# Decode attention over paged rows: one lookup and two transfers per cached page, issued by pairs, with the rope keys gathered from the rows and turned on chip

## The reference

```python
ckv = jnp.concatenate([cache_ckv_l[pages].reshape(past, KV_LORA), ckv_new], axis=0)   # 2048 + 8 rows of 256
kpe = jnp.concatenate([cache_kpe_l[pages].reshape(past, QK_ROPE), kpe_new], axis=0)   # 2048 + 8 rows of 32
k_nope = jnp.einsum('...lc,chd->...lhd', c_kv, w_uk)                                  # 8 heads of 64
k = rmsnorm(jnp.concatenate([k_nope, k_rope], axis=-1), k_head_norm)                  # k_rope: kpe, the same for all heads
s = jnp.einsum('qhd,khd->hqk', q, k) * SCALE                                          # then causal mask, softmax p
o_lat = jnp.einsum('hqk,kc->qhc', p, c_kv)
```

## Time and profile before

| | |
|---|---|
| median of 3 runs | 1536.07 us (1535.14 to 1537.04) |
| the profiled execution, its own time | 1533.52 us |
| span of that execution, first to last instruction | 1531.5 us |
| mean granted TensorE clock | 0.994 of 2.4 GHz |
| decode loop, first page product to last key scores | 706.8 to 1017.5 us |
| products of TensorE, instructions | 10771 |
| transfers on SP's queue | 139.97 MB in 244498 packets |

### The profile page before, as it was taken

The page is one execution under the profiler, slowest core; times in us unless marked ns, Lnnn a source line. Parts: engine busy times, 40 slices in busy tenths (PEclk is TensorE's granted clock), DMA queues, the critical chain, the costliest instruction groups (busy, mean ns, idle before and its releaser), DMA issues.

```text
span 1531.5 us, 31143 instructions
## 1 busy us (share of the span) xinstructions
PE 1491.3 (97%) x10771; PEld 1434.9 (94%) x10771; DVE 1067.9 (70%) x1738; ACT 655.5 (43%) x1215; POOL 454.3 (30%) x463
## 2 busy tenths in 40 slices
PE   8999999999999999999999888999999999999999
PEld 8999999999999999588888888888999999999999
DVE  7999898421269975865888788854759998985000
ACT  6444445322221242464666666642434444445111
POOL 4000002454465744320344333223551000005432
PEclk9999999999999999999999999999999999999999
DMA  6233234222333651003444443432222332332322
GB/s 176 70 103 103 82 97 116 78 83 75 82 83 100 83 116 47 13 4 99 129 127 129 124 125 111 128 106 72 83 83 56 109 97 85 106 92 81 91 77 82
DMA packets 245460, 141.69 MB, mean 93 GB/s; under 512 B 22705, under 2 KB 242290, under 8 KB 245362
## 3 DMA queue, kind: packets, MB, share of 16 engines
q1 hardware_dynamic: 244498, 139.97, 33.1%
q10 hardware_dynamic: 864, 0.48, 0.1%
HBM read 136.82 MB, written 3.58 MB: 92 GB/s over the span
## 4 chain that ended last, share of the span: by engine, by line
PE 52%; issue 24%; SPq 11%; POOL 7%; DVE 3%; ACT 1%; DMA 1%; POOLq 0%; DVEq 0%; ACTq 0%
PE ps L493 28%; PE ps L1522 14%; POOL w_lobuf L468 7%; SPq L726 3%; SPq L731 3%; SPq L742 3%; SPq L737 2%; PE ps L1861 2%; PE ps L1647 1%; PE ps L1701 1%; PE ps L1676 1%; PE ps L479 1%; PE ps L1691 1%; DMA w_rawbuf<-in_ffn_w_gu 1%; DVE cT_lo L2466 1%
## 5 line engine op out<-in xcount | busy, mean ns | idle before, releaser
L468 POOL TENSOR_TENSOR w_lobuf<-w_rawbuf,w_hibuf 128x256 fp32r<-128x256 f32 (+1 forms) x328 | 316.4, 996 | 801.4 <-ACT w_hibuf L461 801.3
L1522 PE MATMUL ps<-xs,w 128*128 128x288 f32 x3192 | 427.7, 296 | 0.8 <-DVE w L1984 0.8
L1522 PEld LDWEIGHTS ps<-xs,w 128*128 128x128 f32 x3192 | 426.8, 188 | 1.5 <-issue 1.5
L461 ACT ACTIVATE w_hibuf<-w_rawbuf 128x1024 fp32r<-128x1024 f32 (+1 forms) x89 | 104.4, 1173 | 353.3 <-PE ps L493 332.9
L2192 DVE SCALAR_TENSOR_TENSOR xT<-ps,xT 128x576 f32<-128x576 f32 x23 | 17.4, 756 | 202.4 <-PE ps L493 202.4
L1984 DVE TENSOR_TENSOR w<-w_raw,w 128x512 fp32r<-128x512 f32 x228 | 154.0, 690 | 0.3 <-ACT w L1029 0.2
L493 PE MATMUL ps<-a_hi,w_lobuf 128*128 128x288 f32 x682 | 147.5, 297 | 0.0
L493 PE MATMUL ps<-a_hi,w_hibuf 128*128 128x288 f32 x682 | 147.2, 296 | 0.0
L493 PE MATMUL ps<-x_hi,w_hibuf 128*128 128x288 f32 x656 | 142.2, 298 | 4.1 <-POOL w_lobuf L468 2.9
L493 PE MATMUL ps<-a_lo,w_hibuf 128*128 128x288 f32 x682 | 145.5, 294 | 0.0
L493 PE MATMUL ps<-x_lo,w_hibuf 128*128 128x288 f32 x656 | 140.8, 296 | 0.0
(11 more groups left out here) (335 smaller groups left out, 2602.6 us busy)
## 6 DMA issues: line engine op xcount, KB each, us to landing
w_raw<-in_ffn_w_gu SPq DMA_DIRECT2D x76, 256.0 KB, 2.9
up_rows<-in_ffn_w_gu SPq DMA_DIRECT2D x72, 256.0 KB, 3.2
c_nat<-in_pages_in SPq DMA_DIRECT2D x128, 144.0 KB, 2.2
c_ring<-in_pages_t SPq DMA_DIRECT2D x128, 128.0 KB, 2.1
w_rawbuf<-in_w_in SPq DMA_DIRECT2D x58, 256.0 KB, 3.2
w_rawbuf<-in_ffn_w_down SPq DMA_DIRECT2D x32, 384.0 KB, 4.0
w_rawbuf<-in_ffn_w_down SPq DMA_DIRECT2D x32, 320.0 KB, 3.4
w_rawbuf<-in_ffn_w_gu SPq DMA_DIRECT2D x24, 256.0 KB, 3.4
```

The lines of the kernel that those rows point to most:

```text
L461: act.activation(w_hibuf[:, r % HIS, 0:size], w_rawbuf[:, r, 0:size], ACT.Copy).then_inc(w_hi_done, 1)
L468: ins = pool.tensor_tensor(w_lobuf[:, r, part], w_rawbuf[:, r, part], w_hibuf[:, r % HIS, part].bitcast(F32), ALU.subtract)
L1522: mm = pe.matmul(ps[:, seven_bank(f, slot), 0:HALF], m, xs[:, slot, n, k, :], start=k == 0 and j == 0, stop=k == KH - 1 and j == 2)
```

## The change

SP's `load_pages` by groups becomes `load_pair` by pairs: two lookups, two ring issues, two row issues. The ring issue of pair pp waits for the low part of pair pp-2, the row issue for the pair's own use count. The transposed rope keys are no longer an input, and their 128 transfers go. Sequence 0 keeps the page numbers that it has looked up: 16 lookups for 16 pages.

Instead, VectorE copies the rope values of a group's four pages out of `c_nat` into `kpe_rows` (128 x 128), behind the two sums of iteration 2g; TensorE transposes them behind page 4g+2 (behind page 3 in the first group of sequence 0) into bank `PEB`; ScalarE copies them into `kpeT` behind the squares of that page; the key scores wait for that copy. GpSimd's squaring of a sequence waits for the last of its four gathers. The counts of the semaphores follow.

```diff
-        def kpe_page(s, g):
-            return 3 if at(s, g) == (0, 0) else 4 * g + 1
+        def kpe_page(s, g):
+            return 3 if at(s, g) == (0, 0) else 4 * g + 2
...
-            def load_pages(s, b, used=None):
-                for g in range(NP // 4):
-                    found = [page_of(s, 4 * g + u) for u in range(4)]
-                    sp.wait_ge(ct_lo, s * PAIRS + (2 * g - 2))
-                    load_ring(g, found)
-                    sp.wait_ge(pe_scored, s * (NP // 4) + (g - 1))
-                    load_kpe(g, found)
-                    if used is not None:
-                        sp.wait_ge(pages_used, used + 2 * (g + 1))
-                    load_rows(b, g, found)
...
+            def load_ring(pp, two):
+                for u, page in enumerate(two):
+                    sp.dma_start(c_ring[:, (2 * pp + u + RING // 2) % RING, :], pages_t[ds(page, 1), :, :].rearrange("a p c -> (a p) c")).then_inc(ring_in[pp % 2], 16)
+            def load_rows(b, pp, two):
+                for u, page in enumerate(two):
+                    sp.dma_start(c_nat[:, b, 2 * pp + u, :], pages_in[ds(page, 1), :, :].rearrange("a p c -> (a p) c")).then_inc(nat_in[b][pp // 2], 16)
+            def load_pair(s, b, pp, used=None):
+                two = [page_of(s, 2 * pp + u) for u in range(2)]
+                sp.wait_ge(ct_lo, s * PAIRS + (pp - 1))
+                load_ring(pp, two)
+                if used is not None:
+                    sp.wait_ge(pages_used, used + (pp + 1))
+                load_rows(b, pp, two)
...
             sp.wait_ge(rows_done, 2 * NT + PT_TILES)
+            early = [[page_of(0, 2 * pp + u) for u in range(2)] for pp in range(2)]
+            for pp in range(2):
+                load_ring(pp, early[pp])
             sp.wait_ge(prep_q, 1)
+            for pp in range(2):
+                load_rows(0, pp, early[pp])
+            later = [[page_of(0, 2 * pp + u) for u in range(2)] for pp in range(2, 4)]
+            for pp in range(2, 4):
+                load_rows(0, pp, later[pp - 2])
             sp.wait_ge(prep_tr, 2)
             sp.wait_ge(uk_split, 1)
+            for pp in range(2, 4):
+                sp.wait_ge(ct_lo, pp - 1)
+                load_ring(pp, later[pp - 2])
+            for pp in range(4, PAIRS):
+                load_pair(0, 0, pp)
             sp.wait_ge(prep_mm, 2)
+            for pp in range(PAIRS):
+                load_pair(1, 1, pp)
             with sp.Fori(1, NS // 2) as i:
                 for b in range(2):
+                    for pp in range(PAIRS):
+                        load_pair(i * 2 + b, b, pp, i * (2 * PAIRS) + (EARLY_PAIRS + PAIRS * (b - 2)))
...
                 for g in range(NP // 4):
                     pool.wait_ge(nat_in[b][g], uses * 64)
+                pool.wait_ge(kpe_row, s * 4 + 4)
                 k = c_nat[:, b, :, KL:KL + DR]
...
+            def kpe_copy(s, g):
+                act.wait_ge(pe_tr, s * 4 + (g + 1))
+                if not (isinstance(s, int) and s == 0 and g < 2):
+                    act.wait_ge(pe_scored, s * 4 + (g - 1))
+                act.activation(kpeT[:, g % 2, :], ps[:, PEB, 4 * HQ:4 * HQ + P], ACT.Copy).then_inc(pe_copied, 1)
...
                         act.activation(sq[:, u, 0:H * DN].rearrange("p (g c) -> p g c", g=2), ps[:, n:n + 2, k_cols(b)], ACT.Square).then_inc(page_sq, 1)
+                        if t == kpe_page(s, t // 4):
+                            kpe_copy(s, t // 4)
...
+            def kpe_transpose(s, b, g, uses):
+                pe.wait_ge(kpe_row, s * 4 + (g + 1))
...
+                    pe.wait_ge(scores_read, s * 4 + g)
+                pe.transpose(ps[:, PEB, 4 * HQ:4 * HQ + P], kpe_rows[:, :, :].rearrange("p t d -> p (t d)"), ident[:, :]).then_inc(pe_tr, 1)
             def kpe_scores(s, g):
-                pe.wait_ge(kpe_in[g % 2], (s * 2 + (g // 2 + 1)) * 64)
...
+                pe.wait_ge(pe_copied, s * 4 + (g + 1))
...
                         mm.then_inc(page_mm, 1)
                         if prev and stacked(s) and t == NP - 1:
                             next(soft)
+                        if t == kpe_page(s, g):
+                            kpe_transpose(s, b, g, uses)
...
+                    if pp % 2 == 0:
+                        g = pp // 2
+                        dve.wait_ge(nat_in[b][g], uses * 64)
+                        if not (isinstance(s, int) and s == 0 and g == 0):
+                            dve.wait_ge(pe_tr, s * 4 + g)
+                        dve.tensor_copy(kpe_rows[:, :, :], c_nat[:, b, 4 * g:4 * g + 4, KL:KL + DR]).then_inc(kpe_row, 1)
                     if pp % 2:
                         g = pp // 2
                         dve.wait_ge(pe_scored, s * 4 + (g + 1))
```

More of the change, by code:

```diff
@@ L91, in constants, with layer @@
     return {"ident": ident, "causal": causal, "rope": rope, "new_mask": new}
-def layer(nc, x_t, cols_in, pages_t, pages_in, pages_k, state_conv, page_table, w, const, out):
+def layer(nc, x_t, cols_in, pages_t, pages_in, state_conv, page_table, w, const, out):
     ctx = ExitStack()
@@ L223, in layer @@
         c_ring = place("c_ring", [P, RING, KL], F32, S3)
+        kpe_rows = place("kpe_rows", [P, 4, DR], F32, ring_at + 8 * DK * P + 8192 + 8 * (SQ + KN + SQ))
         kpeT = place("kpeT", [P, 2, P], F32, rstd_at)
@@ L726, in page_of @@
                 return sp.value_load(pages[0:1, ds(s * NP + t, 1)], min_val=0, max_val=pages_t.shape[0] - 1)
[L728 to L737, removed]
@@ L739, in load_kpe @@
[L739 to L754 removed]
+            def load_ring(pp, two):
+                for u, page in enumerate(two):
+                    sp.dma_start(c_ring[:, (2 * pp + u + RING // 2) % RING, :], pages_t[ds(page, 1), :, :].rearrange("a p c -> (a p) c"))\
+                        .then_inc(ring_in[pp % 2], 16)
@@ L756, in _ @@
             sp.wait_ge(rows_done, 2 * NT + PT_TILES)
-            found = [page_of(0, u) for u in range(4)]
-            load_ring(0, found)
-            load_kpe(0, found)
+            early = [[page_of(0, 2 * pp + u) for u in range(2)] for pp in range(2)]
+            for pp in range(2):
+                load_ring(pp, early[pp])
             sp.wait_ge(prep_q, 1)
-            load_rows(0, 0, found)
-            for g in (1, 2):
-                load_rows(0, g, [page_of(0, 4 * g + u) for u in range(4)])
+            for pp in range(2):
+                load_rows(0, pp, early[pp])
@@ L764, in _ @@
+            later = [[page_of(0, 2 * pp + u) for u in range(2)] for pp in range(2, 4)]
+            for pp in range(2, 4):
+                load_rows(0, pp, later[pp - 2])
             sp.wait_ge(prep_tr, 2)
             sp.wait_ge(uk_split, 1)
-            found = [page_of(0, 4 + u) for u in range(4)]
-            load_ring(1, found)
-            load_kpe(1, found)
-            load_rows(0, 3, [page_of(0, 12 + u) for u in range(4)])
-            for g in (2, 3):
-                found = [page_of(0, 4 * g + u) for u in range(4)]
-                sp.wait_ge(ct_lo, 2 * g - 2)
-                load_ring(g, found)
-                sp.wait_ge(pe_scored, g - 1)
-                load_kpe(g, found)
+            for pp in range(2, 4):
+                sp.wait_ge(ct_lo, pp - 1)
+                load_ring(pp, later[pp - 2])
@@ L2750, in laid_out @@
     return {"x_t": rows.T, "cols_in": np.concatenate([*gains, taps], axis=1), "pages_t": pages_t,
-            "pages_in": np.concatenate([ckv, kpe], axis=2), "pages_k": kpe.transpose(0, 2, 1)}
+            "pages_in": np.concatenate([ckv, kpe], axis=2)}
 def state_first(state):
```

16 lines of the change are left out of this document (7 added, 9 removed).

## The result

| | before | after |
|---|---|---|
| median, runs of one chip | 1535.61 us (1533.72 to 1537.04) | 1558.83 us (1557.57 to 1562.40) |
| ratio to before | | 1.0156, 95% interval 1.0134 to 1.0177 |
| span of the profiled execution | 1531.5 us | 1558.1 us |
| mean granted TensorE clock | 0.994 | 0.990 |

The account below looks back on a forecast made before the run. SP's always-busy queue was not taken as the bound: most TensorE waits came from other engines. Costs of 19.3 us less gains of 10.2 gave +9.1 on the median 1536.07, so 1545.2 us; range 1528 to 1556.

Parts of the forecast that it names:

- SP really was the bound: Rival: SP's queue bounds the decode loop; decides if VectorE gathers before page 4g+2 ends on TensorE; 1529 us, chance 0.2.
- SP's relief: Decode loop: SP, with fewer issues, stops being late, and TensorE waits led back to it go; gain 10.2 us.
- fold waits: TensorE's two long waits for the fold, 2.08 and 1.80 us, shrink to 0.6 each; gain 2.7 us.
- half clock: Slow TensorE products at 1.2 GHz behind the first long fold wait (833 to 870 us) go; gain 1.2 us.
- small waits: Small TensorE waits behind late ring pages elsewhere in the loop go; gain estimated at 1.0 us.
- Its wait shrinks by 3 us ... 5.3 us: Sequence 7: ScalarE's merge-weight wait shrinks 3 us; TensorE's 3.1 us den_sum wait and 2.2 us of half clock go.
- my 994.4: Sequence 7: forecast time, in us, when SP issues the first merge weights, instead of 995.91.
- The stalls in sequences 1 to 6: TensorE waits before transposes for VectorE's gather, behind the sums: 2.7 us a sequence, 16.2 in all.
- For sequences 1 to 6 I take the same: Extends the 2.7 us of stalls to all six sequences; layer-norm in 5 and 6 delays VectorE but TensorE's present waits are larger.
- third rival: Slower by more: two stalls a sequence bring TensorE's 1.2 GHz level, 8.4 us more, 1554 us, chance 0.12.
- Sequence 7: only g=1, 1.5: In the last sequence only group 1's transpose stalls TensorE, waiting for its gather; cost 1.5 us.
- the rule: VectorE copies share ports with GpSimd: a gather could wait over 1 us, only g=3 near; some 3 us, outside the sum.

Follow-up runs that it names:

- experiment 3: Changed kernel without gather, transposes and copy-out, keys zero, SP still issuing by pairs: 1529.11 us, ratio 0.9956 to the kernel before.
- experiment 6: Kernel before, SP by groups, without its rope-key transfers and TensorE's wait for them, keys zero: 1527.61 us, ratio 0.9943.
- experiment 5: Kernel before, with ScalarE's split of the first merge weight one iteration later in the last sequence: 1530.28 us, ratio 0.9972.
- experiment 1: Changed kernel with VectorE's gather moved to the head of its iteration, right behind the low part: 1544.71 us, ratio 1.0057.
- Experiment 2: Changed kernel with ScalarE's split of the first merge weight one iteration later in sequence 7, gather unmoved: 1552.08 us, ratio 1.0104.
- 8: Changed kernel, early gather, transposes and copies-out one page earlier, split unmoved, SP issuing first merge weights behind pair 4 of sequence 7: 1538.46 us.
- 4: Changed kernel with both the gather at the head of its iteration and the merge-weight split one iteration later: 1536.20 us, ratio 1.0002.
- 7: Changed kernel with early gather, later merge-weight split, and all transposes and copies-out one page earlier: 1537.93 us, ratio 1.0012.
- 9: Changed kernel, early gather, later merge-weight split, transposes and copies-out one page earlier except group 1's: 1537.22 us, ratio 1.0003.
- experiment 11: Changed kernel, early gather, later merge-weight split, but gathers alone: no transposes or copies-out, keys zero: 1535.00 us, ratio 0.9991.
- 12: Changed kernel, later split, transposes and copies-out one page earlier except group 1's, no gathers, rows to be turned zero: 1530.66 us, ratio 0.9972.
- 10: Changed kernel without gather, transposes and copy-out, keys zero, and the merge-weight split one iteration later: 1527.64 us, ratio 0.9944.

## Why the prediction was right in sign and wrong in size

**What bounds the kernel: right, and shown.** SP's queue held 70% of the chain, yet emptying it gained 6.6 us (experiment 3) or 8.7 (experiment 6), not a tenth of the loop. The rival "SP really was the bound" (1529 us) fails on its own condition: VectorE had not gathered in time.

**SP's relief: 6.6 us instead of 10.2.** The parts outside sequence 7 (fold waits 2.7, half clock 1.2, small waits 1.0: 4.9) measured 4.1 us: sequences 1 to 6 take 232.0 us before and 227.9 in experiment 3. In sum they were nearly right, but not one by one. The fold wait of 2.08 us in sequence 3 fell to 0.54, and its half clock went; that of 1.80 in sequence 5, which I had called the same, stayed at 1.65 without any key issue, so its 1.2 us were no gain: sequence 5 took 41.3 us before and 41.1 in experiment 3.

The step that failed is "Its wait shrinks by 3 us ... 5.3 us". I let SP issue the weight right behind low part 5. In experiment 3 low part 5 is done at 989.53 and the weight leaves at 994.35, because pair 6 and the lookups of pair 7 hold SP. That this is 0.05 us from my 994.4 is luck: mine was in the time of the kernel before (and its own terms, 991.3 + 2.1 + 1.5, give 994.9), and against the end of sequence 6 the weight left no earlier than before (24.9 us, 24.7). I also let ScalarE arrive later by delays that were themselves costs. The wait went from 6.06 only to 5.13, and sequence 7 gained 1.9 us. In the changed kernel, with those delays, it was 3.90, near my 3, and den_sum's wait did go; the copy-out's, 6.29, came in its place. The size of the prize was right (experiment 5), its cause was not in the change.

**The hop on TensorE, VectorE and ScalarE as work: right.** In the changed kernel the gather took 0.22 us (forecast 0.25), the transpose 0.27 to 0.33, the copy-out 0.27 (0.31).

**The stalls in sequences 1 to 6.** The mechanism is shown by experiment 1: move the gather, and they go. The places and sizes:

| group | forecast | sequence 3 |
|---|---|---|
| 0 | about 0, absorbed | 0.57 |
| 1 | 1.5 | 1.47 |
| 2 | about 0, absorbed | 1.52 |
| 3 | 1.1 | 1.27 |

Against the kernel without keys, sequences 1 to 4 cost 2.5 us each, where 2.7 were forecast. The stalls sum to 4.8; about half took the place of waits that were there before. So the total was right though two of four terms were set to zero: their waits are real, and the waits they displaced paid for them; that this came out at the forecast is luck in part. That they cost nothing by themselves can't be read from this; the sum of 2.5 is what is shown.

**Sequences 5 and 6: 3.5 and 4.4 us instead of 2.7 each.** "For sequences 1 to 6 I take the same" failed. I had named the layer-norm work on VectorE and offset it against "TensorE's present waits". In sequence 5 it stands straight ahead of the gather:

```profile
917.33 0.85 DVE L2571 TENSOR_TENSOR ln_acc<-ln_acc,y 128x576 f32<-128x576 f32 x1
918.10 1.27 DVE L2655 TENSOR_REDUCE page_ss<-sq 128x8 f32<-128x512 f32 x2
919.29 0.21 DVE L2663 COPY kpe_rows<-c_nat 128x128 f32<-128x128 f32 x1
```
```profile
919.56 0.33 PE L1826 MATMUL ps<-ident,kpe_rows 128*128 128x128 f32 x1 [2.29 <-DVE kpe_rows L2663]
```

2.29 is the 1.47 of the other sequences plus these 0.85, and behind it the granted clock is 0.63 from 920 to 923 us. That is the third rival (1554, chance 0.12), in two sequences of seven: the windows of 0.86 over 12 us in 5 and 0.88 over 14 us in 6 are 3.4 us each at 1.2 GHz.

**Sequence 7 is the failure: +7.1 where -3.8 was forecast, 10.9 of the 13.1 us that the loop was off.** 3.4 is the merge weight's gain that did not come; 7.4 is the key path, which cost 8.9 us against experiment 3 where "Sequence 7: only g=1, 1.5" was written. Three of its four groups stalled, 1.57, 1.83 and 1.01 us before the transposes at 998.06, 1007.04 and 1015.86. Softmax steps or not, the sums of the iteration alone keep the gather late. And I put the merge split and the copy-out in separate paragraphs and never in one list. The copy-out belongs to page 10, the split stands behind page 9, on the same engine; the rows that show its 6.06 us wait were on my table, and I asked only which wait the change would shorten, not which instruction it would now put behind it. Experiment 2 gives 6.7 us for that alone. It is also an interaction: the same late weight costs 5.6 us in the trace where the next pair's high part is what matters behind it (experiment 5), and nothing where SP issues it early (8).

**Smaller terms.** Sequence 0: 1.2 us against 1.6. "GpSimd's squaring now waits ...: nothing" holds, though GpSimd waited 27.7 us in all: no engine is shown waiting for these squares.

**Gather and GpSimd.** The sum left out that a gather could wait for a GpSimd instruction. In the changed kernel it happened to one of 32. VectorE's timeline and GpSimd's in sequence 5:

```profile
941.03 0.74 DVE L2663 COPY kpe_rows<-c_nat 128x128 f32<-128x128 f32 x1
941.69 0.68 DVE L2475 TENSOR_TENSOR cT_lo<-c_ring,cT_hi 128x512 fp32r<-128x512 f32 x1
```
```profile
939.35 2.34 POOL L928 TENSOR_TENSOR c_lo<-c_nat,c_hi 128x512 fp32r<-128x512 f32 x2 [1.23 <-ACT c_hi L1324]
941.94 1.33 POOL L956 TENSOR_TENSOR c_nat<-c_nat 128x512 f32<-128x512 f32 x1 [0.25 <-DVE kpe_rows L2663]
```

The gather that began beside the subtraction took 0.74 us instead of 0.22, and ended 0.08 us after it; one at 858.28, begun 0.08 after such a pair's end, took 0.21. This agrees with the Trainium skill ("SBUF — State Buffer", "Who interferes with whom"), by which a VectorE copy can contend with GpSimd for the ports that they share. In the changed kernel it cost 0.5 us once, where I had priced the rule at some 3. With the gather moved (experiments 1, 4, 7 to 9 and 11) six or seven of the 32 took 1.2 us, some 6 to 7 us more on VectorE: twice the price that I had put on the rule, and nearly all in group 1, not in group 3, where I had placed it.

**What stays open.** The early gather costs 7.4 us by the medians. The collision with GpSimd and the wait for the maximum behind it are read from the traces, but no run takes them away: a gather placed early and clear of the subtraction was not tried. The wide spread of experiment 11 (8 us between its runs) goes with the granted clock of the whole run: 0.998 in the run of 1530.65 us, 0.992 in that of 1538.58. The difference is 2 x 0.006 x 1536 = 18 us more at 1.2 GHz, which can cost up to 9 us, an estimate. Why one execution gets more of it than another stays open.

## What to carry to other kernels

When work moves onto an engine's hand-written list, write out for each moved instruction all that stands ahead of it in every peeled or special iteration, and ask of each wait in the list what new instruction comes to stand behind it: here 0.27 us of copying behind a 3.9 us wait cost 6.7 us. A queue that is always busy and fills the chain of waits may still be worth only half a per cent; leave the suspected work out and time it before replacing it. And judge a fix by the time, not by the wait it removes: waits on the key path fell from 14.8 to 4.2 us between two kernels of equal time. Then look again at how long the moved instruction itself takes in its new place: here 1.2 us instead of 0.22, once in each of six sequences.

## What the runs showed of the hardware that was not expected

- The length of a wait did not decide by itself whether TensorE's clock fell. Four waits of 0.57 to 1.52 us in 40 us left the granted clock at 1.00 (823 to 863 us after, 35.1 us busy of 40); one of 2.29 was followed by 0.63 for the next 3 us, and one of 6.29 by 0.74 over 20 us. But before the fold of sequence 5, waits of 1.54 to 1.71 us were followed by 3.4 us at 1.2 GHz in experiments 1, 4, 7, 8, 9, 11 and 12 (0.79 over 8 us in each), and waits of 1.65 (3), 1.66 (10) and 1.80 us (before) were not. The 2.08 us before the fold of sequence 3 brought it in the kernel before, and 2.31 us at the same place in experiment 5 did not (1.00 from 850 to 870 us):

```profile
854.18 0.38 PE L1790 MATMUL ps<-o_lat,fold 128*128 128x1 f32 x2 [2.31 <-DVE o_lat L2532]
```

- A VectorE copy of 128x128 values, rows of 32 strided out of four pages, takes 0.22 us, as long as the copy of 64 columns did, but 1.21 us beside GpSimd's subtraction (experiment 11). It is the time to the next instruction's start that is smaller still: the low part behind it starts 0.13 us later (798.45, 798.58).
